# A hybrid backbone step on one core: the even layer's cumulative log gates by a prefix scan on VectorE

## The reference, cut to what matters

```
qa, ia, zf, zb, ga, qb, kb, vb = split_cols(h @ w_in, EVEN_SPLITS)
logf = log(lb + (1 - lb) * sigmoid(z));  key = (1 - lb) * sigmoid(-z)      # once forward, once backward
cum = jnp.cumsum(logf, axis=2)                                              # within a chunk
scores = einsum('bnthk,bnshk,bntshk->bnhts', q, k, exp(cum_t - cum_s))      # causal within the chunk
kv = einsum('bnshk,bnshv->bnhkv', k * jnp.exp(last[:, :, None] - cum), v)
state' = exp(last) * state + kv;   o = scores @ v + (q * exp(cum)) @ state
```

## Time and profile before

| what | value |
|---|---|
| median of 3 runs | 1143.74 us (1143.3 to 1143.93) |
| the profiled execution's own time | 1141.77 us |
| its span | 1139.6 us |
| PE busy | 981.8 us (86%) |
| DVE busy | 291.4 us (26%) |
| ACT busy | 195.5 us (17%) |
| DMA, mean over the span | 284 GB/s |
| granted TensorE clock, mean | 0.955 |

### The profile page before, as it was taken

How to read it: one execution, slowest core, us unless ns; L and a number is a source line. 1 busy time by engine, 2 the same in 40 slices (tenths; PEclk the granted TensorE clock), 3 DMA queues, 4 the chain that set the end, 5 groups by cost and what they waited for, 6 DMA issues and landing times.

```text
span 1139.6 us, 13423 instructions
## 1 busy us (share of the span) xinstructions
PE 981.8 (86%) x5665; PEld 528.6 (46%) x5665; DVE 291.4 (26%) x644; ACT 195.5 (17%) x348; POOL 24.8 (2%) x45
## 2 busy tenths in 40 slices
PE   3799999989899786886699999999997998968873
PEld 1475454454466444552244444444444654535541
DVE  1310236722642111110402222231006312111103
ACT  1111122250311000010112122353003110000001
POOL 2000000000000000000000011000000000000000
PEclk9999999989899998998889999999998899989987
DMA  9999729983169999999954444046341499999992
GB/s 303 395 348 370 301 84 391 409 343 119 53 237 366 415 416 418 415 416 416 387 187 148 155 152 182 28 148 239 148 153 68 173 368 416 419 416 414 417 417 97
DMA packets 77794, 323.28 MB, mean 284 GB/s; under 512 B 4892, under 2 KB 4948, under 8 KB 61092
## 3 DMA queue, kind: packets, MB, share of 16 engines
q1 hardware_dynamic: 74756, 312.78, 69.7%
q0 software_dynamic: 2976, 9.61, 2.4%
HBM read 316.34 MB, written 6.03 MB: 283 GB/s over the span
## 4 chain that ended last, share of the span: by engine, by line
PE 65%; DMA 21%; DVE 6%; SPq 4%; ACT 2%; issue 2%; DVEq 0%
PE PS L595 62%; DMA ring<-in_moe_w_gate 11%; DMA ring<-in_moe_w_down 8%; SPq L502 3%; DMA ring<-in_mod_w 2%; DVE H L1519 1%; DVE scratch L1509 1%; PE PS L641 1%; SPq L469 1%; ACT L1199 0%; DVE scratch L1544 0%; DVE X L1546 0%; ACT scratch L1197 0%; SPq L488 0%; DVE scratch L1723 0%
## 5 line engine op out<-in xcount | busy, mean ns | idle before, releaser
L595 PE MATMUL PS<-ring,scratch 128*32 128x256 f32 (+4 forms) x2720 | 306.8, 464 | 83.0 <-DMA ring<-in_moe_w_gate 35.2
L595 PEld LDWEIGHTS PS<-ring,scratch 128*32 128x32 f32 (+2 forms) x2720 | 150.9, 128 | 236.8 <-issue 201.4
L595 PE MATMUL PS<-ring,HT 128*128 128x512 f32 x576 | 253.5, 596 | 3.8 <-issue 2.7
L595 PEld LDWEIGHTS PS<-ring,HT 128*128 128x128 f32 x576 | 108.7, 191 | 135.5 <-issue 132.6
L595 PE MATMUL PS<-scratch 128*128 128x512 f32 (+2 forms) x440 | 117.1, 437 | 4.4 <-issue 1.5
L595 PEld LDWEIGHTS PS<-scratch 128*128 128x128 f32 (+1 forms) x440 | 56.0, 193 | 59.9 <-issue 55.8
L595 PE MATMUL PS<-scratch,H 128*128 128x128 f32 x640 | 82.4, 284 | 0.0
L1922 DVE TENSOR_TENSOR scratch<-PS,scratch 128x256 f32<-128x256 f32 x20 | 8.5, 425 | 287.4 <-ACT scratch L1350 287.4
L595 PEld LDWEIGHTS PS<-scratch,H 128*128 128x128 f32 x640 | 77.3, 198 | 9.2 <-issue 9.2
L595 PE MATMUL PS<-ring,cpad 128*32 128x512 f32 x384 | 46.9, 628 | 14.0 <-DMA ring<-in_mod_w 14.0
L1350 ACT ACTIVATE scratch<-PS 128x256 f32<-128x256 f32 x20 | 7.7, 384 | 268.5 <-PE PS L595 268.5
(11 more groups left out here) (272 smaller groups left out, 620.0 us busy)
## 6 DMA issues: line engine op xcount, KB each, us to landing
ring<-in_moe_w_gate SPq DMA_DIRECT2D x56, 1024.0 KB, 18.2
ring<-in_moe_w_up SPq DMA_DIRECT2D x56, 1024.0 KB, 20.5
ring<-in_moe_w_down SPq DMA_DIRECT2D x56, 1024.0 KB, 19.3
ring<-in_mod_w SPq DMA_DIRECT2D x24, 2048.0 KB, 16.6
ring<-in_odd_w_in SPq DMA_DIRECT2D x12, 2048.0 KB, 14.0
ring<-in_even_w_in SPq DMA_DIRECT2D x7, 2048.0 KB, 15.3
ring<-in_moe_w_gate SPq DMA_DIRECT2D x4, 2048.0 KB, 15.0
ring<-in_moe_w_up SPq DMA_DIRECT2D x4, 2048.0 KB, 12.9
```

The source lines that it names most:

```text
L595: return nc.tensor.matmul(out, lhsT, rhs, start=start, stop=stop, skip_group_check=True, **kw)
```

## The change

The three kinds of sums no longer come from PE. After queries are made (third chunk), DVE runs `sums()`: a prefix scan along the tokens with a constant that resets at every chunk's start, in place for the forward gates; for the backward gates a scan and two subtractions. LF now holds one row of 512 per stream and direction. Per group, `centred` and `to_edge` make the two other sums by a subtraction from a broadcast column, `centred` and `to_edge` of group 0 at once behind `sums()`, those of a later group within the group before it. ACT takes four exponentials from SBUF instead of three from PSUM. On PE the transposes of the gates, the sums and `keep_warm` are gone; two more late blocks are moved forward, between the halves of the last chunks, in the weight stream too, and a group has fewer fillers. On DVE the squares of queries and keys move from group 2 to group 1, and `norm_qk(1)` from group 3 to behind the groups. The constant `cums` gives way to `within` and `resets` of the same total size.

```diff
@@ -67,7 +67,7 @@
         items.append(("even_in", c))
-        if i in MOD_BANK:
+        if i in MOD_BANK or i in (4, 5):
             l, b = late.pop(0)
@@ -173,7 +173,7 @@
         _evend = _at
-        LF = H[:, :, :, :].rearrange("p s k c -> p (s k c)").rearrange("p (d h t) -> p d h t", d=2, h=HA)
+        LF = H[:, :, :, :].rearrange("p s k c -> p (s k c)").rearrange("p (s d h t) -> p s d h t", s=S, d=2, h=HA)
         SG = ST.rearrange("p a n -> p (a n)")[:, 0:1024].rearrange("p (h t) -> p h t", h=HA)
@@ -724,68 +722,45 @@
                 s, d = g // 2, g % 2
-                pe.wait_ge(lf_ready, d + 1)
-                if g:
-                    pe.wait_ge(masked_ready, g)
-                else:
-                    pe.wait_ge(in_free_v, 2)
-                for h in range(HA):
-                    mm = nc.tensor.transpose(PS[:, 4, P * h:P * h + P], LF[:, d, h, P * s:P * s + P], ident)
-                mm.then_inc(lft_done, 1)
                 if g >= 2:
                     pe.wait_ge(decayed_ready, g)
                     late_mod(5)
                 else:
+                    pe.wait_ge(in_free_v, 2)
                     half_chunk()
-                pe.wait_ge(lft_ready, g + 1)
-                if g:
-                    pe.wait_ge(states_ready, g)
-                else:
-                    pe.wait_ge(mod_ready, 5)
-                for h in range(HA):
-                    mm = matmul(PS[:, h, 0:3 * P], LFT[:, h, :], cums_c[:, d, :], True, True)
-                mm.then_inc(cums_done, 1)
-                if g < 2:
-                    half_chunk()
-                else:
-                    pe.wait_ge(mod_ready, 2 * g + 4)
-                    keep_warm(5, 5)
-                pe.wait_ge(qk_ready, 4 * (g + 1))
+                pe.wait_ge(qk_ready, 4 * g + 2)
                 for h in range(HA):
                     mm = matmul(PS[:, 4, P * h:P * h + P], E1N[:, h, :], E1[:, h, :], True, True)
                 mm.then_inc(scores_done, 1)
-                if g < 2:
-                    pe.wait_ge(in_free_v, 2)
+                pe.wait_ge(qk_ready, 4 * g + 3)
+                if g:
+                    pe.wait_ge(mod_ready, 2 * g + 4)
                 for h in range(HA):
                     mm = nc.tensor.transpose(PS[:, 5, P * h:P * h + P], E23[:, h, P:2 * P], ident)
                 mm.then_inc(decayed_turned, 1)
-                if g == 0:
+                if g < 2:
                     half_chunk()
-                elif g == 1:
-                    pe.wait_ge(half_read, 6)
-                    late_mod(7)
                 pe.wait_ge(decayed_ready, g + 1)
                 if g == 0:
                     pe.wait_ge(in_free_a, 3)
+                    pe.wait_ge(mod_ready, 5)
                 for h in range(HA):
                     for n in range(NSUB):
                         mm = matmul(PS[:, n, P * h:P * h + P], K2[SUB * n:SUB * n + SUB, h, :],
                                     IV[SUB * n:SUB * n + SUB, s, P * h:P * h + P], True, True)
                 mm.then_inc(kv_done, 1)
-                if g == 0:
+                late_mod(5)
+                if g < 2:
                     half_chunk()
-                elif g == 1:
-                    late_mod(7)
-                else:
-                    late_mod(5)
                 pe.wait_ge(masked_ready, g + 1)
                 if g == 2:
-                    pe.wait_ge(mod_ready, 7)
+                    pe.wait_ge(half_read, 6)
                 for h in range(HA):
                     matmul(PS[:, 6 + s, P * h:P * h + P], LFT[:, h, :], IV[:, s, P * h:P * h + P],
                            d == 0 and h == 0, False)
                 pe.wait_ge(states_ready, g + 1)
+                pe.wait_ge(qk_ready, 4 * g + 4)
                 order = list(range(NSUB)) if d == 0 else list(range(NSUB))[::-1]
@@ -1228,13 +1203,15 @@
                     d = 0 if c == ZF else 1
-                    A_(LF[:, d, :, :], byhead, SIGMOID).then_inc(f_ready, 1)
+                    A_(LF[:, :, d, :, :].rearrange("p s h t -> p h s t"),
+                       byhead.rearrange("p h (s t) -> p h s t", s=S), SIGMOID).then_inc(f_ready, 1)
                     A_(KEYT[:, d, :, :], byhead, SIGMOID, scale=-1.0).then_inc(in_free_a, 1)
                 elif c == QA:
                     A_(SG[:, :, :], byhead, SIGMOID).then_inc(f_ready, 1)
                     for d in range(2):
                         act.wait_ge(key_ready, 2 * d + 1)
-                        A_(LF[:, d, :, :], LF[:, d, :, :], LN).then_inc(lf_ready, 1)
+                        lf = LF[:, :, d, :, :].rearrange("p s h t -> p s (h t)")
+                        A_(lf, lf, LN).then_inc(lf_ready, 1)
                 else:
@@ -1257,23 +1234,24 @@
             for g in range(4):
+                act.wait_ge(cums_done, 2 * g + 1)
+                A_(E1N[:, :, :], E1[:, :, :], EXP, scale=-1.0).then_inc(exps_ready, 1)
+                A_(E1[:, :, :], E1[:, :, :], EXP).then_inc(exps_ready, 1)
+                act.wait_ge(cums_done, 2 * g + 2)
+                A_(E23[:, :, P:2 * P], E23[:, :, P:2 * P], EXP).then_inc(exps_ready, 1)
+                if g:
+                    act.wait_ge(group_done, g)
+                A_(E23[:, :, 0:P], LF[:, g // 2, g % 2, :, :], EXP).then_inc(exps_ready, 1)
                 if g == 0:
                     first_half(QB)
-                elif g == 1:
-                    first_half(GA)
-                act.wait_ge(cums_done, g + 1)
-                if g:
-                    act.wait_ge(group_done, g)
-                A_(E1[:, :, :], PS[:, 0:4, 0:P], EXP).then_inc(exps_ready, 1)
-                A_(E1N[:, :, :], PS[:, 0:4, 0:P], EXP, scale=-1.0).then_inc(exps_ready, 1)
-                A_(E23[:, :, :], PS[:, 0:4, P:3 * P], EXP).then_inc(exps_ready, 1)
-                if g == 1:
-                    act.wait_ge(used, AT[("even_in", GA)] + 1)
-                    A_(GS[:, 1, :], PS[:, 7, :], SILU).then_inc(half_read, 1)
                 act.wait_ge(decayed_turned, g + 1)
                 A_(K2[:, :, :], PS[:, 5, :].rearrange("p (h k) -> p h k", h=HA), COPY).then_inc(decayed_ready, 1)
                 if g == 0:
                     first_half(KVB)
+                elif g == 1:
+                    first_half(GA)
+                    act.wait_ge(used, AT[("even_in", GA)] + 1)
+                    A_(GS[:, 1, :], PS[:, 7, :], SILU).then_inc(half_read, 1)
                 elif g == 2:
@@ -1587,6 +1565,39 @@
+            def sums():
+
+                for d in range(2):
+                    dve.wait_ge(lf_ready, d + 1)
+                    for s in range(S):
+                        lf = LF[:, s, d, :, :].rearrange("p h t -> p (h t)")
+                        part = lf if d == 0 else LFT[:, :, :].rearrange("p h t -> p (h t)")
+                        st.link(V.tensor_tensor_scan(part, cst("resets"), lf, 0.0, ALU.mult, ALU.add))
+                        if d:
+                            before = K2[:, :, :].rearrange("p h t -> p (h t)")
+                            st.link(V.tensor_tensor(before, part, lf, ALU.subtract))
+                            lf, part, before = (x.rearrange("p (b t) -> p b t", t=SUB) for x in (lf, part, before))
+                            st.link(V.tensor_tensor(lf, bcast(part[:, :, SUB - 1:SUB], [P, HA * NSUB, SUB]), before,
+                                                    ALU.subtract))
+
+            def blocks(g):
+                return LF[:, g // 2, g % 2, :, :].rearrange("p h (n t) -> p h n t", t=SUB)
+
+            def centred(g):
+
+                mid = SUB // 2 - 1 + g % 2
+                cum = blocks(g)
+                V.tensor_tensor(E1.rearrange("p h (n t) -> p h n t", t=SUB), cum,
+                                bcast(cum[:, :, :, mid:mid + 1], [P, HA, NSUB, SUB]), ALU.subtract).then_inc(cums_done, 1)
+
+            def to_edge(g):
+
+                edge = 0 if g % 2 else SUB - 1
+                cum = blocks(g)
+                V.tensor_tensor(E23[:, :, P:2 * P].rearrange("p h (n t) -> p h n t", t=SUB),
+                                bcast(cum[:, :, :, edge:edge + 1], [P, HA, NSUB, SUB]), cum, ALU.subtract)\
+                    .then_inc(cums_done, 1)
+
@@ -1615,6 +1626,9 @@
                                            op0=ALU.mult, op1=ALU.mult).then_inc(in_free_v, 1)
+                    sums()
+                    centred(0)
+                    to_edge(0)
                 else:
@@ -1668,45 +1682,43 @@
                 ts = slice(P * s, P * s + P)
-                dve.wait_ge(lft_done, g + 1)
-                if g:
-                    dve.wait_ge(group_done, g)
-                V.tensor_copy(LFT[:, :, :].rearrange("p h k -> p (h k)"), PS[:, 4, :]).then_inc(lft_ready, 1)
+                last = SUB - 1 if d == 0 else 0
+                dve.wait_ge(exps_ready, 4 * g + 1)
+                V.tensor_tensor(E1N[:, :, :], E1N[:, :, :], KEYT[:, d, :, ts], ALU.mult).then_inc(qk_ready, 1)
+                dve.wait_ge(exps_ready, 4 * g + 2)
```

(74 more changed lines are left out.)

## The result

The changed kernel takes 1132.39 us (median of 4 runs, 1129.92 to 1133.33) against 1143.52 before (4 runs, 1142.84 to 1143.93): ratio 0.9902, 95% interval 0.9886 to 0.9917, faster by 11.1 us. The prediction was 1132.0. The profiled execution took 1131.86 us (span 1129.7; before 1141.77 and 1139.6); for it the sum had said 1130.1.

A forecast was written before the change was run, and what follows sets the result against it. PE's own instructions were taken to bound the groups, transfers the experts. Stall 8.9 plus clock 2.0 less 22.6 gave -11.7 us: 1130.1 for the profiled execution, 1132.0 for the median, range 1127 to 1139.

The forecast's parts named there:

- PE bound in the groups, its instructions are the time: In the four groups, work that leaves PE leaves the time; with the hand-over, 22.6 us less.
- The stall ahead of the fourth chunk: PE waits for a modrow addition behind DVE's scans and subtractions, going on at 109.5 instead of 100.62: 8.9 us lost.
- The clock behind it: After the stall ahead of the fourth chunk PE runs at a lower clock: 2.0 us lost, ends 0 and 3.
- The hand-over and the transfers: Hand-over to attention takes 5.5 us, DVE's rotation coming 2.1 us later; nothing added for transfers.
- 3.5 us of cover: Last late-block item lands 83 us from group 0's start, PE wants it at 86.5; no transfer wait added.
- the prediction's own signs of being wrong: Clock under 1.00 from group three, PE waiting for late-block transfers, scans beyond 2.5 us, or gain gone by first expert weights.
- One to one to the end: A gain in the even layer carries whole through the transfer-bound experts, which begin some 12 us earlier.
- What was costed at nothing: ACT's four exponentials, covered by fillers, and squares moved into group 1, where DVE is idle two thirds: no cost.
- The stall that doesn't come: Rival: scans ahead of the fourth chunk lie under other work, PE's 22.6 us gain stays whole: 1121.1 us; chance 0.04.
- DVE in all groups: Rival: each group shows 2 us of DVE-ACT round trip, 8 us go (late transfer looks the same): 1140; chance 0.10.
- Slower through the clock: Rival: without constant matmuls PE falls to 1.2 GHz in groups 2 and 3, costing 25 us: 1157; chance 0.07.
- Scans at 4 us: Rival: scans cost three times the price, the stall ahead of the fourth chunk grows 11 us: 1143; chance 0.06.

The follow-up runs named there:

- third experiment: Changed kernel with the five constant matmuls put back on PE in groups 2 and 3: 1135.53 us, 3.9 slower than the changed kernel.
- first experiment: Changed kernel with scans and group 0's subtractions on DVE moved behind the third chunk's late-block addition to modrow: 1118.59 us, ratio 0.98.
- second experiment: Changed kernel with ten constant matmuls on PE in the stall ahead of the fourth chunk: 1128.93 us, ratio 0.9883.
- e8_skipped_code: Changed kernel with 42 small matmuls written into the overflow block PE jumps over, so never executed: 1132.37 us, ratio 0.9927.
- last two experiments: The changed kernel with 42 added matmuls, as e9_hidden_code (1135.43 us) and as e8_skipped_code (1132.37 us).
- e1_sums_behind: The first experiment: changed kernel with scans and group 0's subtractions behind the late block's addition to modrow: 1118.59 us, ratio 0.98.
- e9_hidden_code: Changed kernel with 42 small matmuls in lots of 14 ahead of three places where PE waits for expert weights: 1135.43 us, ratio 0.9946.
- e2_warm_in_stall: The second experiment: changed kernel with ten constant matmuls on PE in the stall ahead of the fourth chunk: 1128.93 us, ratio 0.9883.

## Why the prediction was right, and where two terms were off

*PE bound in the groups, its instructions are the time.* Right. 28.8, 28.8, 12.9 and 13.8 were foreseen, 28.90, 28.78, 12.89 and 13.34 came. The third experiment shows it from the other side for group 2. But the 0.6 us that group 3 was given for waiting on the block's addition to modrow did not come. PE idled 1.13 us there, 0.69 of it in a wait for ACT that group 2 has too and that the kernel before had in both, 0.23 for a transfer and 0.21 for DVE's last state:

```profile
206.89 1.17 PE L593 MATMUL PS<-scratch 32*128 32x128 f32 x32 [0.69 <-ACT scratch L1248]
213.37 1.08 PE L593 MATMUL PS<-scratch,E 128*32 128x128 f32 x32 [0.21 <-DVE small L1739]
```

*The stall ahead of the fourth chunk.* Right: 8.9 foreseen, 8.97 measured, and the first experiment took it away. The scan, bounded by 0.73 and 1.25 from start to start and taken at 1.25, has 1.26. The estimate by the Trainium skill, page "DVE: opcode table, instruction layouts, handler registers and perf-mode slots", section "Datapath and trigger behaviour", half throughput for the scan, agrees: 1.22 us against 0.69 for a product or sum of the same size. The rule of the Trainium skill, page "VectorE: DVE Perf Modes", section "The DRAIN you can't avoid", that a semaphore costs nothing extra, again does not: the linked subtraction at 104.60 holds the next for 0.72 us, the unlinked one at 108.76 for 0.61.

*The clock behind it.* 2.0 foreseen, 2.26 measured, 2.26 given back by the second experiment.

*The hand-over and the transfers.* Wrong in size. The 5.5 us held what DVE's moved norm costs, and DVE was done at 219.59, about when the block would have ended without late items. The failing step is "3.5 us of cover". The stream began where it was put (47 us from the origin at 130.47; it is idle from 174 and busy at 178), but the last of seven items landed 90.4 us from the origin, not 83, and PE wanted it at 87.3. (The prediction says 86.5, but its own group times, 84.3, and the 3.0 us from there to the block's second half make 87.3 too.) From the start to the last landing it is 43.4 us, 6.2 for each item and not 5.1. The DMA view of the changed kernel, 177.47 to 220.87 us and (last row) 120 to 172 us, has what the step left out:

```profile
q1 hardware_dynamic: 3953, 15.73, 92.2%
q0 software_dynamic: 320, 1.05, 6.1%
...
ring<-in_even_w_in SPq DMA_DIRECT2D x2, 2048.0 KB, 8.0
```

POOL's queue (q0) moves 1.05 MB in between, 2.6 us at 406 GB/s. The ring's queue (q1) moves 15.73 MB, and the seven items are 14.68: another 1.05 MB, again 2.6 us, belongs to items behind them and had moved before the last of the seven landed. Both queues together need 41.3 of the 43.4 us; the other 2.1 lie at the start, where the first bytes come late. That is 7.3 of the 7.4 us. A transfer with little ahead of it shows start and landing in one: 8.0 us from issue to landing, 2.9 more than its share of the stream. The price was 3.1 us of waiting and the clock after it: +4.5 in the hand-over. PE waiting for transfers of late blocks was one of the prediction's own signs of being wrong, and here it came.

*One to one to the end.* The transfers did follow PE, with a share of 1.00 at 406 GB/s from 320 us on. But the sign named for it, experts that begin some 12 us earlier, did not come: the last write of X ahead of them is at 278.55 instead of 284.78, 6.2 us. The end of the first experts gave 3.85 us more that the sum did not have, by a wait for instructions that depends on the code's position. The trace of before has that wait, put down to "issue", but nothing in it says that it would go. So the median came out within 0.4 us of the forecast because +4.5 and -3.85 nearly cancel, and that is luck; for the profiled execution the sum was 1.8 short.

*What was costed at nothing.* ACT's four exponentials and the squares moved into group 1 showed nowhere: PE never idled in groups 0 and 1.

*The rivals.* The stall that doesn't come: it came, and without it the kernel has 1118.6, the neighbourhood of the 1121.1 given. DVE in all groups: only 0.85 and 1.13 us of PE's time idle in groups 2 and 3, most of it for ACT, none in 0 and 1; its twin, a transfer that comes late, did come once. Slower through the clock: 1.00 in all groups. Scans at 4 us: 1.22.

## What to carry to other kernels

Work that leaves the bound engine for an idle one is free only behind the idle engine's next obligation: the same scans cost some 11 us of stall and lower clock ahead of a small addition that the bound engine waits for, and PE waits for none of them behind it. When a stage gets faster, recompute when each weight must have landed, with the time from issue to landing, all other queues and the items behind it in the sum; without its earlier blocks this change was worth nothing. A difference of a few us far from the edit can be code position: compare the waits for "issue" before explaining it.

## What was not expected of the hardware

Behind a jump over a long block PE waited 3.51 to 3.56 us with a load of instructions in the wait, in four kernels, and not at all in the traces of the other ten runs. The changed kernel, which doesn't have it, differs from `e8_skipped_code`, which has it, only in code that is never executed. In the kernel before and in the last two experiments the eight matmuls behind it took 5.40 us, at a granted clock of 0.67 in the mean (558.22 to 563.45 before) where the changed kernel has 1.00. That cost nothing here, because the changed kernel waits for DVE among the same matmuls: from the first write of X behind the experts to the next layer's first weights (559.59 to 570.99 before, 549.50 to 560.91 after) both take 11.4 us.

A wait of 3.10 us was followed by sixteen matmuls in 3.52 us, one of 2.77 (`e1_sums_behind`) by the same in 1.92, but one of 2.73 (`e9_hidden_code`) by 2.67, and one of only 2.35 (`e2_warm_in_stall`) by 3.51. The length of the wait alone does not tell whether the clock falls.
